# Reciprocal root mean squares by ScalarE's square root and one Newton step on VectorE

## The reference

```python
def rms_norm(x, g):
    y = x * lax.rsqrt(jnp.mean(x * x, axis=-1, keepdims=True) + EPS)   # EPS = 1e-6
    return y * g

# in each layer's mixer
q  = (rms_norm(cq, mla_q_norm) @ w_q_up)        # low rank, 256 wide
kv = (rms_norm(ckv, mla_kv_norm) @ w_kv_up)     # low rank, 128 wide
q, k = rms_norm(q, mla_q_qknorm), rms_norm(k, mla_k_qknorm)    # 8 heads of 96
ck_q, ck_k = rms_norm(ck_q, ...), rms_norm(ck_k, ...)          # 4 heads of 64
merged = concat(rms_norm(o_sb), rms_norm(o_mla), rms_norm(o_ck)) @ w_out

# in the second block
y = rms_norm(y.reshape(b, s, 8, 256), ssd_norm_g)     # gated rows
qn, kn = rms_norm(q, q_norm_g), rms_norm(k, k_norm_g) # 3 groups of 8 heads of 64
```

## Time and profile before

| | us |
|---|---|
| median of 3 runs | 2313.06 |
| lowest and highest | 2312.45, 2314.32 |
| the profiled execution's own time | 2303.63 |
| its span in the profile | 2301.8 |

### The profile page before, as it was taken

The page is one execution under the profiler, slowest core; times in us unless marked ns, Lnnn a source line. Parts: engine busy times, 40 slices in busy tenths (PEclk is TensorE's granted clock), DMA queues, the critical chain, the costliest instruction groups (busy, mean ns, idle before and its releaser), DMA issues. The chain is left out here.

```text
span 2301.8 us, 28168 instructions
## 1 busy us (share of the span) xinstructions
PE 2050.5 (89%) x11131; PEld 1739.5 (76%) x11131; DVE 1714.4 (74%) x2350; ACT 1295.4 (56%) x1853; POOL 0.2 (0%) x4
## 2 busy tenths in 40 slices
PE   6877999985689999999999999879878688889989
PEld 4746778864688787878878787679767578878987
DVE  5765888656659999998998989778584555567873
ACT  2354543345458777777777776566415344455652
POOL 0000000000000000000000000000000000000000
PEclk9987999996789999999999999989999798989999
DMA  7721688730029998998999998555303343224543
GB/s 301 261 93 55 224 326 320 282 117 37 37 73 359 352 349 332 363 349 328 358 349 341 342 362 313 217 211 177 109 20 128 119 138 103 98 92 147 185 165 108
DMA packets 70091, 497.20 MB, mean 216 GB/s; under 512 B 8000, under 2 KB 8256, under 8 KB 10688
## 3 DMA queue, kind: packets, MB, share of 16 engines
q1 hardware_dynamic: 69664, 494.28, 58.3%
q10 hardware_dynamic: 288, 1.05, 0.1%
HBM read 494.25 MB, written 1.05 MB: 215 GB/s over the span
## 5 line engine op out<-in xcount | busy, mean ns | idle before, releaser
L337 DVE TENSOR_TENSOR wlo<-ring,whi 128x1024 fp32r<-128x1024 f32 (+2 forms) x845 | 1016.6, 1216 | 318.0 <-ACT whi L385 295.5
L385 ACT ACTIVATE whi<-ring 128x1024 fp32r<-128x1024 f32 (+2 forms) x845 | 886.6, 1055 | 583.4 <-PE ps L235 501.7
L235 PE MATMUL ps<-whi,hT 128*128 128x256 f32 (+3 forms) x928 | 321.4, 346 | 38.1 <-DVE hTl L291 12.7
L235 PE MATMUL ps<-wlo,hT 128*128 128x256 f32 (+3 forms) x928 | 315.9, 340 | 0.0
L235 PE MATMUL ps<-whi,hTl 128*128 128x256 f32 (+3 forms) x928 | 315.5, 340 | 0.0
L235 PE MATMUL ps<-whi,xg 128*128 128x512 f32 (+1 forms) x768 | 293.0, 382 | 5.2 <-DVE wlo L337 4.9
L235 PE MATMUL ps<-whi,xgl 128*128 128x512 f32 (+1 forms) x768 | 289.0, 376 | 0.0
L235 PE MATMUL ps<-wlo,xg 128*128 128x512 f32 (+1 forms) x768 | 288.9, 376 | 0.0
L235 PEld LDWEIGHTS ps<-whi,hT 128*128 128x128 f32 x928 | 183.6, 198 | 63.5 <-DVE wlo L337 16.9
L235 PE MATMUL ps<-whi,hf 128*128 128x512 f32 x528 | 212.7, 403 | 12.5 <-DVE ffn_w L291 6.4
L235 PE MATMUL ps<-wlo,hf 128*128 128x512 f32 x528 | 210.1, 398 | 0.0
(11 more groups left out here) (279 smaller groups left out, 2697.5 us busy)
## 6 DMA issues: line engine op xcount, KB each, us to landing
ring<-in_wstream SPq DMA_DIRECT2D x462, 1024.0 KB, 4.9
ring<-in_wstream SPq DMA_DIRECT2D x4, 832.0 KB, 5.7
ring<-in_wstream SPq DMA_DIRECT2D x6, 256.0 KB, 2.6
cst<-in_cst SPq DMA_DIRECT2D x1, 1028.0 KB, 8.9
x<-in_x SPq DMA_DIRECT2D x1, 1024.0 KB, 14.4
work<-in_bias ACTq DMA_DIRECT2D x2, 512.0 KB, 5.5
ring<-in_wstream SPq DMA_DIRECT2D x2, 512.0 KB, 4.5
out_x<-x SPq DMA_DIRECT2D x1, 1024.0 KB, 4.0
```

Of the source, the lines that this page charges most:

```text
L235: i = self.e.matmul(out, lhsT, rhs, start=start, stop=stop, skip_group_check=True)
L337: i = self.e.tensor_tensor(K.wlo[:, q % NS, 0:cols], src, hi.bitcast(F32), ALU.subtract)
L385: i = self.e.activation(K.whi[:, q % NS, 0:cols], K.ring[:, m % RING, at:at + cols], ACT.Copy)
```

## The change

All twelve calls of `rstd` (four in each of two layers, the gate, three window groups) take the second way. `rstd` on VectorE shrinks from twelve instructions to four: a reciprocal of the root that ScalarE has written, and one Newton step. It now waits for ScalarE's root. The squares carry a scale, so that their sums are already means. The extra doubling at `low` goes. ScalarE gets one `ACT.Sqrt` for each place (`act_roots`, with EPS as a bias from a new column). At the head norms it also gets one dummy Sqrt before, and one dummy Exp behind; at the merged rows one dummy Sqrt before the last squares; at `low` and the gate no dummy.

```diff
@@ Vector
+    def rstd(self, y, ms, n, root, key=None):
+        t = self.K.r_t[:, 0:n]
+        self.wait_ge(self.K.act, root)
+        self.recip(y, self.K.sd[:, 0:n])
+        self.stt(t, ms, EPS, y, ALU.add, ALU.mult)
+        self.stt(t, t, -0.5, y, ALU.mult, ALU.mult)
+        self.stt(y, t, 1.5, y, ALU.add, ALU.mult, key=key)
@@ new
+def act_roots(K, a, n, key):
+    a.act(K.sd[:, 0:n], K.ssq[:, 0:n], ACT.Sqrt, bias=K.col("eps"), key=key)
-def act_root_ahead(K, a):
-    a.act(K.sd[:, 2:3], K.cst("ones")[:, 0:1], ACT.Sqrt, own=False)
+def act_root_ahead(K, a, fn=ACT.Sqrt):
+    a.act(K.ahead[:, 0:1], K.cst("ones")[:, 0:1], fn, own=False)
@@ act_head_norms
-        a.act(sq, w, ACT.Square, key=(s, "sq", u), own=False)
+        a.act(sq, w, ACT.Square, scale=d ** -0.5, key=(s, "sq", u), own=False)
+    act_root_ahead(K, a)
+    a.wait_ge(K.dve, (s, "ss", len(vs) - 1))
+    act_roots(K, a, n * len(vs), (s, "sd"))
+    act_root_ahead(K, a, ACT.Exp)
@@ act_mixer
+    act_roots(K, a, 4, (s, "low", "sd"))
     act_gained(K, a, (s, "low"), K.low, 3, ...)
...
     turn(6)
+    act_root_ahead(K, a)
     act_merged_squares(K, a, s, (1,))
+    act_roots(K, a, 6, (s, "merged", "sd"))
@@ dve_mixer
-    v.wait_ge(K.act, (s, "lowss"))
-    v.ts(K.ssq[:, 2:4], K.ssq[:, 2:4], 2.0, None, ALU.mult)
-    v.rstd(K.rs[:, 0:4], K.ssq[:, 0:4], 4, 256)
+    v.rstd(K.rs[:, 0:4], K.ssq[:, 0:4], 4, (s, "low", "sd"))
@@ act_gated
+    act_roots(K, a, 16, "ysd")
```

More of the change, by code:

```diff
@@ L1151, in dve_head_norms @@
     m = n * len(vs)
-    v.rstd(K.rs[:, 0:m], K.ssq[:, 0:m], m, d, key=(s, "rs"))
+    v.rstd(K.rs[:, 0:m], K.ssq[:, 0:m], m, (s, "sd"), key=(s, "rs"))
     v.last()
@@ L1284, in act_mixer @@
     for i in range(2):
-        a.act(K.sbuf2[:, 0:256], K.proj[:, i, CQ:CQ + 256], ACT.Square, accum=K.ssq[:, i:i + 1])
-        a.act(K.sbuf2[:, 0:128], K.proj[:, i, CKV:CKV + 128], ACT.Square, accum=K.ssq[:, 2 + i:3 + i], key=(s, "lowss") if i else None)
+        a.act(K.sbuf2[:, 0:256], K.proj[:, i, CQ:CQ + 256], ACT.Square, scale=1.0 / 16, accum=K.ssq[:, i:i + 1])
+        a.act(K.sbuf2[:, 0:128], K.proj[:, i, CKV:CKV + 128], ACT.Square, scale=128 ** -0.5, accum=K.ssq[:, 2 + i:3 + i])
+    act_roots(K, a, 4, (s, "low", "sd"))
     act_gained(K, a, (s, "low"), K.low, 3, lambda j: K.col(f"mq{l}", j) if j < 2 else K.col(f"mkv{l}"))
@@ L1336, in act_merged_squares @@
             a.act(K.sbuf2[:, 0:c1 - c0], K.xn[:, i, c0:c1], ACT.Square, accum=K.ssq[:, 3 * i + n:3 * i + n + 1],
-                  scale=1.0 if c1 - c0 == 256 else float(np.sqrt(0.5)), key=(s, "oss") if i and n == 1 else None)
+                  scale=(c1 - c0) ** -0.5)
 def dve_mixer(K, v, l):
@@ L1401, in dve_mixer @@
     values(6)
-    v.wait_ge(K.act, (s, "oss"))
-    v.rstd(K.rs[:, 0:6], K.ssq[:, 0:6], 6, 256)
+    v.rstd(K.rs[:, 0:6], K.ssq[:, 0:6], 6, (s, "merged", "sd"))
     for i in range(2):
@@ L2267, in act_gated @@
         for g in range(8):
-            a.act(K.sbuf2[:, 0:256], K.X[:, i, 256 * g:256 * g + 256], ACT.Square, accum=K.ssq[:, 8 * i + g:8 * i + g + 1],
-                  key="yss" if i and g == 7 else None)
+            a.act(K.sbuf2[:, 0:256], K.X[:, i, 256 * g:256 * g + 256], ACT.Square, scale=1.0 / 16, accum=K.ssq[:, 8 * i + g:8 * i + g + 1])
+    act_roots(K, a, 16, "ysd")
     for n0, n, use in row_groups(K, a, "gs", KT):
@@ L2285, in dve_gated @@
     v.split_to(K.parts["gs"][0] + NS - 1)
-    v.wait_ge(K.act, "yss")
-    v.rstd(K.rs[:, 0:16], K.ssq[:, 0:16], 16, 256)
+    v.rstd(K.rs[:, 0:16], K.ssq[:, 0:16], 16, "ysd")
     for i in range(2):
@@ L2700, in memory @@
         K.r_t = sb("r_t", [128, 32])
-        K.r_i = sb("r_i", [128, 32], I32)
         K.nm3, K.den3, K.rd3, K.lse3, K.wt3 = (sb(n, [128, 3, 2, 8]) for n in ("nm3", "den3", "rd3", "lse3", "wt3"))
@@ L2713, in memory @@
         K.along = K.cbm.rearrange("p b t -> p (b t)")
-        K.sd = sb("sd", [128, 4])
+        K.sd = sb("sd", [128, 32])
+        K.ahead = sb("ahead", [128, 1])
         aux = sb("aux", [128, 2560])
@@ L2845, in pack_cols @@
     out[:, a:a + 16] = (10000.0 ** (-np.arange(0, 32, 2, dtype=np.float64) / 32)).astype(np.float32)[None]
+    out[:, COLS["eps"][0]] = EPS
     a = COLS["router"][0]
```

## The result

| | median us | lowest to highest | runs |
|---|---|---|---|
| before | 2312.76 | 2310.66 to 2316.62 | 6 |
| changed | 2290.02 | 2287.55 to 2291.28 | 6 |

The account below looks back on a forecast made before the run. The prediction took the mixers to be bound by their own chains and the experts by the weight stream. Its terms, 2 x (-1.46 - 1.28 + 0.1) + 0.0 - 0.6 - 1.35, gave -7.3: 2305.8 us, range 2300.8 to 2310.8.

Parts of the forecast that it names:

- The experts run at the speed of the stream: Experts between the mixers: the weight stream sets their pace, yet time saved on a mixer's own chain should stay saved.
- `low`: Norm at `low`, twice: ScalarE's root plus four VectorE instructions take 1.13 us in place of 2.59, so -1.46 each.
- `merged`: Norm of merged rows, twice: 1.14 us in place of 2.42, table load hidden in ScalarE's idle time, so -1.28 each.
- `ckn` and `mln`: Two head norms per layer: VectorE gains 1.32 us at `ckn`, but late ScalarE lengthens its wait at `mln`; together +0.1.
- gate: Gate norm: load, root, handover and four instructions take 2.48 us in place of 2.52, so 0.0.
- `qk0`: Head norm `qk0`: the chain ends at 1830.61 in place of 1831.25, so -0.6 us.
- window group 0: First exponential of window group 0: the Exp table load leaves the chain, standing behind `qk0` instead, so -1.35 us.
- `qk1`, `qk2`: Norms of the later window groups: TensorE's projection is on the chain, so VectorE's gain is worth nothing, 0.0.
- dear loads: Rival, chance 0.13: table loads at each `mln`, gate and `qk0` cost twice 1.30 us; only -2.1, giving 2311.0.
- the slower rival: Rival, chance 0.04: back-to-back table loads stall at `mln`, gate and `qk0`; at 4.5 us a load, 2318.6 us.
- The rival of the stream: Rival, chance 0.05: weight ring not full at the mixers' ends, so their 5.3 us are lost in the experts; 2311.1.
- The clock: Rival, chance 0.17, either side: places starting sooner meet another TensorE clock level, 4 us less or more; 2301.8 or 2309.8.

## Why the prediction was wrong, point by point

**The step that failed is a term that the sum put at nothing without a reason:** every stage without a line of the edit at the time that it had, the experts above all. The diff held the sign of it: a column more in a table, one tile dropped, one grown, one new. I read these as bookkeeping. The column moved `hT` and the work area, which hold the large operands of TensorE other than the split weights, by 32 bytes. The experts then took 811.0 us in place of 824.6, and 811.8 in the old code at the new addresses. The last down-projection, whose pitch fell in the same way, took 61.3 in place of 63.4. With 32 bytes and no line of the edit the old kernel saved 15 us.

**A premise was wrong beside it.** "The experts run at the speed of the stream" was read from the DMA digits. The window shows what bounds them: TensorE is busy for 397.4 of 400 us. When its matmuls came closer, the stream went from 347 to 353 GB/s and the other engines followed. With the right reading the pitch of 233 ns, which stands almost three thousand times in the experts, would have been the number to ask about, though nothing in the trace of the kernel before says that it can be 227.

**The terms of the sum** held, one by one (to two digits the sum is -7.23 and not -7.25; with the values measured it is -6.9, and the edit alone measured -6.0, between -2.3 and -9.7):

| place | forecast | measured, changed kernel |
|---|---|---|
| `low`, each | -1.46 | 1.14 for 2.59: -1.45 |
| `merged`, each | -1.28 | 2.67 for 3.93: -1.26 |
| `ckn` and `mln`, each layer | +0.1 | 15.66 for 15.56: +0.10 |
| gate | 0.0 | 2.55 for 2.51: 0.0 |
| `qk0` | -0.6 | 3.03 for 3.43: -0.4 |
| window group 0 | -1.35 | 0.10 for 1.38: -1.28 |
| `qk1`, `qk2` | 0.0 | the projections stayed on the chain |

38 loads ran, each of 1.28 us, as forecast, and in the rows above what follows a load begins 0.01 to 0.02 behind its end. So dear loads and the slower rival, which rests on them, are out. The rival of the stream is out too: the experts took 825.0 us in the new code at the old addresses and 824.6 and 824.0 in the kernel before, so at most 1 us of the mixers' 5.3 can have been given back. The Trainium skill says in "ScalarE: Activation LUTs", section "What ACT_TABLE_LOAD costs", that a switch costs 2.66 with a drain of 1.38; the trace doesn't agree: in the rows above the root begins at 1770.31, 0.02 behind the end of its load (1769.01 + 1.28 = 1770.29). One sentence of the prediction contradicts its own working: "at `mln` the multiply 3.8 us behind the end of the squares, not 3.7 as now". The working gave 138.66 - 135.86 = 2.8; measured are 137.98 - (133.25 + 1.70) = 3.03. That the term of `ckn` and `mln` came out at +0.10 is in part luck: the squares of `mln` were late by 0.77 (12.63 behind the sums of `ckn`, before 11.86) and not by 1.0, and the chain behind them took 0.2 more than the 2.8 of the working. From the row of the last squares:

```profile
133.25 1.70 ACT L365 ACTIVATE aux<-work 128x768 f32<-128x768 f32 x2 [0.28 <-DVE ssq L298]
```

The term of `qk0` was 0.2 too large for the same reason: 0.1 of idle time between the dummy and the root, and a reciprocal that took 0.35 (of 32 columns) where those of 2 and 4 columns took 0.17 and 0.18.

**The clock** did act as the rival said, and small. In the new code with old addresses the first matmuls behind layer 0's norm `nf` stand 0.43 apart, at a granted clock of 0.50 in the 3 us before and 0.75 in the 4 us from 216:

```profile
216.26 0.63 PE L235 MATMUL ps<-whi,hT 128*128 128x512 f32 x1
216.69 0.63 PE L235 MATMUL ps<-wlo,hT 128*128 128x512 f32 x1
```

512 columns in 0.43 us is the lower level of 1.2 GHz. The kernel before had 0.30 there and then 0.23. In the changed kernel the sixteen matmuls of layer 1 in the earlier trace rows took 3.65 in place of 1.97. It moves a place by 1 to 2 us. Such differences can't be told from others between two traces: in the old kernel alone the start with mixer 0 differs by 2.8 and mixer 1 by 3.9.

**What stays open.** In the new code with old addresses `xbc` took 3.3 us more, although nothing that it reads had moved. Its pitch is 113.4 ns in both traces of the kernel before and 117.8 in the six others that have `hT` at the same place, old code among them. What selects it is not known; of the 3.7 us that the changed kernel loses there, 3.3 came with any change, and only the rest with `hT`. And the parts don't add up to the whole: 0.9955 times 0.9974 is 0.9929, measured were 0.9899. The difference is 7 us. In the one trace of each kernel the windows and the merge stand out (229.0 changed, 237.7 with the new addresses alone, 229.8 with the edit alone, 230.9 before); no run isolated it. With `hT` left in place the parts do add up: 0.9935 times 0.9974 is 0.9909, measured were 0.9902. Open is also the period of the rule, 256 or 512 bytes.

## What to carry to other kernels

An edit that adds, drops or resizes an on-chip tile can move those behind it: print the addresses of the big matmul operands of both versions before costing "unchanged" code, and test an edit in a copy that keeps them. Take what bounds a stage from the engine that hardly pauses in its window, not from a high DMA digit. Where matmuls of 512 columns in float32 bound the time, try a pad that brings loaded and moving tile to the same start modulo 512 bytes (256 may do, which no run tried); here 32 bytes gave more than twelve rewritten norms.

## What the runs showed of the hardware

In these kernels the pitch of matmuls behind each other at full granted clock depends on where the loaded tile starts relative to the moving one (`whi`, `wlo`). With `whi` at 128 modulo 256:

| loaded tile, start modulo 256 | 96 | 160 | 192 | 224 | 0 | 128 |
|---|---|---|---|---|---|---|
| pitch at 512 columns, ns | 233 | 233 | 233 | 234 | 232 | 227 |

With `whi` at 0 it is 227 at 0 and 232 at 128. In both cases of 227 the starts are equal modulo 512 too. At 256 columns the sign is the other one: with `xg` 120 ns where 512 columns have 227, 119 where the two starts differ by 128, and 117 or 113 in most others (113 to 119 with `hT`). By these figures a kernel with mostly such matmuls would lose by the same start; none was run. The durations of the loads themselves did not change: 187 to 189 ns for `xg` in the four traces asked.

The Trainium skill, "SBUF — State Buffer", section "Who interferes with whom", gives TensorE two read ports, one for the moving operand and one for the weights, and calls them independent. If that means that neither sets the pace of the other, these runs disagree: two operands that start at different remainders cost 6 ns of 233. Whether the ports have part in it was not tried.
